# A third w_lo buffer in both stages of a hybrid decoder layer

## What is computed

```python
h = rms_norm(x, norm1_gain) * (1.0 + scale1) + shift1
proj = h @ w_in
(xa, ya, fq, fk, fv, ff, gq, gk, gv, glow, gg) = jnp.split(proj, ...)
out_a = rg_lru(causal_depthwise_conv(xa, conv_w, conv_b), ...) * jax.nn.gelu(ya)
out_b = forgetting_attention(fq, fk, fv, ff, fox_b_f, fox_q_gain, fox_k_gain)
out_c = gated_linear_attention(gq, gk, gv, glow, gg, ...)
mix = jnp.concatenate([out_a, out_b, out_c], axis=-1) @ w_out
x = x + gate1 * mix
h = rms_norm(x, norm2_gain) * (1.0 + scale2) + shift2
gt, up = jnp.split(h @ ffn_w_gate_up, 2, axis=-1)
x = x + gate2 * ((jax.nn.silu(gt) * up) @ ffn_w_down)
```

## Time and profile before

| | |
|---|---|
| median of 3 runs | 2975.97 us (2973.37 to 2981.22) |
| the profiled execution | 2978.72 us, span 2976.9 us |
| mean granted TensorE clock | 0.975 |
| TensorE busy | 2813.1 us (94%) |
| VectorE busy | 1464.6 us (49%) |
| ScalarE busy | 1185.6 us (40%) |
| GpSimd busy | 1036.4 us (35%) |

### The profile page before, as it was taken

The page is one execution under the profiler, slowest core; times in us unless marked ns, Lnnn a source line. Parts: engine busy times, 40 slices in busy tenths (PEclk is TensorE's granted clock), DMA queues, the critical chain, the costliest instruction groups (busy, mean ns, idle before and its releaser), DMA issues.

```text
span 2976.9 us, 32965 instructions
## 1 busy us (share of the span) xinstructions
PE 2813.1 (94%) x12416; PEld 2209.3 (74%) x12416; DVE 1464.6 (49%) x1876; ACT 1185.6 (40%) x1654; POOL 1036.4 (35%) x488
## 2 busy tenths in 40 slices
PE   8998998888989999999999999999999999999999
PEld 4786876566757787886777777867777777778887
DVE  3968786566554334445443454464445654521111
ACT  3333333343345354444433535454335455332222
POOL 2544454221324332233433222434331122444443
PEclk9999999889989999999999999999999999999999
DMA  7555545626643344444624444445244544423222
GB/s 268 181 157 190 152 140 155 184 82 171 212 130 126 121 122 138 127 152 138 185 82 127 144 139 138 148 149 179 70 142 139 155 147 124 141 92 99 93 99 92
DMA packets 159902, 419.05 MB, mean 141 GB/s; under 512 B 18284, under 2 KB 20604, under 8 KB 156672
## 3 DMA queue, kind: packets, MB, share of 16 engines
q1 hardware_dynamic: 157408, 412.48, 44.2%
q10 hardware_dynamic: 2336, 4.46, 0.4%
HBM read 355.95 MB, written 60.92 MB: 140 GB/s over the span
## 4 chain that ended last, share of the span: by engine, by line
PE 65%; DVE 6%; ACT 3%; issue 3%; DMA 2%; SPq 2%; POOL 1%; ACTq 0%; POOLq 0%; DVEq 0%
PE ff_acc_ps L77 17%; PE ff_acc_ps L78 17%; PE ff_acc_ps L79 17%; PE fa_st_ps L1691 1%; PE fa_s_ps L1665 1%; PE fa_o_ps L1707 1%; PE fa_st_ps L1692 1%; PE fa_s_ps L1666 1%; PE fa_o_ps L1709 1%; PE fa_o_ps L1708 1%; DVE fa_inv_sum L1408 1%; PE fa_st_ps L1744 1%; DVE ff_silu L1371 1%; PE fa_o_ps L1781 1%; SPq L956 1%
## 5 line engine op out<-in xcount | busy, mean ns | idle before, releaser
L1093 POOL TENSOR_TENSOR w_lo<-ff_w_raw,w_hi 128x1024 fp32r<-128x1024 f32 (+1 forms) x326 | 772.6, 2370 | 1614.6 <-PE ff_acc_ps L79 1537.6
L77 PE MATMUL ff_acc_ps<-h_odd_hi,w_hi 128*128 128x512 f32 x1856 | 750.2, 404 | 47.8 <-DVE h_odd_lo L1376 13.3
L78 PE MATMUL ff_acc_ps<-h_odd_lo,w_hi 128*128 128x512 f32 x1856 | 737.4, 397 | 0.0
L79 PE MATMUL ff_acc_ps<-h_odd_hi,w_lo 128*128 128x512 f32 x1856 | 735.9, 396 | 0.0
L1108 ACT ACTIVATE w_hi<-ff_w_raw 128x1024 fp32r<-128x1024 f32 (+1 forms) x326 | 338.8, 1039 | 928.7 <-PE ff_acc_ps L79 714.6
L77 PEld LDWEIGHTS ff_acc_ps<-h_odd_hi,w_hi 128*128 128x128 f32 x1856 | 356.8, 192 | 155.5 <-issue 62.5
L79 PEld LDWEIGHTS ff_acc_ps<-h_odd_hi,w_lo 128*128 128x128 f32 x1856 | 356.4, 192 | 78.0
L78 PEld LDWEIGHTS ff_acc_ps<-h_odd_lo,w_hi 128*128 128x128 f32 x1856 | 357.0, 192 | 72.8 <-issue 1.7
L1401 DVE TENSOR_TENSOR fa_p_lo<-fa_probs,fa_p_hi 128x512 fp32r<-128x512 f32 x240 | 154.4, 644 | 286.8 <-ACT fa_p_hi L1142 286.5
L77 PE MATMUL ff_acc_ps<-ff_a_hi,w_hi 128*128 128x512 f32 x704 | 285.2, 405 | 10.1 <-issue 6.1
L78 PE MATMUL ff_acc_ps<-ff_a_lo,w_hi 128*128 128x512 f32 x704 | 280.1, 398 | 0.0
(11 more groups left out here) (263 smaller groups left out, 4044.1 us busy)
## 6 DMA issues: line engine op xcount, KB each, us to landing
ff_w_raw<-in_w_gate_up SPq DMA_DIRECT2D x176, 512.0 KB, 4.0
w_raw<-in_w_in SPq DMA_DIRECT2D x74, 512.0 KB, 4.2
ff_w_raw<-in_w_down SPq DMA_DIRECT2D x64, 512.0 KB, 3.6
mod_w<-in_w_mod SPq DMA_DIRECT2D x24, 1024.0 KB, 5.3
fa_v<-v_split_dram SPq DMA_DIRECT2D x60, 384.0 KB
ff_w_raw<-in_w_out SPq DMA_DIRECT2D x32, 512.0 KB, 3.9
fa_ks_a<-ka_dram SPq DMA_DIRECT2D x60, 256.0 KB
fa_kt_a<-ka_dram SPq DMA_DIRECT2D x60, 256.0 KB
```

The lines of the kernel that those rows point to most:

```text
L77: nc.tensor.matmul(out, hi, act_hi, start=first, stop=False)
L78: nc.tensor.matmul(out, hi, act_lo, start=False, stop=False)
L79: return nc.tensor.matmul(out, lo, act_hi, start=False, stop=last)
L1093: nc.gpsimd.tensor_tensor(w_lo[:, j % LO, wide], w_raw[:, j % RAW, wide], w_hi[:, j % HI, wide].bitcast(F32), ALU.subtract).then_inc(lo_re ...
```

## The change

LO goes from 2 to 3 in both stages and `w_lo` gets three slots, 4096 more bytes in each partition. `high` and `low` stay as they are, and so do the numbers of all other buffers.

```diff
@@ project_in_and_recur
-    RAW, HI, LO, GB, MW, STAGES = 2, 3, 2, 3, 3, 3
+    RAW, HI, LO, GB, MW, STAGES = 2, 3, 3, 3, 3, 3
@@ mix_and_feed_forward
-    HI, LO, RAW, GB, SB, XR = 3, 2, 3, 2, 2, 12
+    HI, LO, RAW, GB, SB, XR = 3, 3, 3, 2, 2, 12
@@ build
-            ("h_odd_hi", [P, KD, BLK], F32R), ("h_odd_lo", [P, KD, BLK], F32R), ("w_hi", [P, 3, KD * P], F32R), ("w_lo", [P, 2, KD * P], F32R),
+            ("h_odd_hi", [P, KD, BLK], F32R), ("h_odd_lo", [P, KD, BLK], F32R), ("w_hi", [P, 3, KD * P], F32R), ("w_lo", [P, 3, KD * P], F32R),
```

## The result

The changed kernel takes 2986.8 us (median of 15 runs) against 2976.0 us (also 15 runs): a ratio of 1.0035, with a 95% interval of 1.0026 to 1.0044. The change costs about 10.4 us. Forecast were 2975.5 us, with a chance of 0.55 that the difference stays within 0.3%, and a range of 2958 to 2989 us. The time lies inside the range, but the forecast change was -0.5 us. The profiled execution of the changed kernel took 2986.6 us, with a span of 2984.8 us, 7.9 us more than the one before.

A forecast was written before the change was run, and what follows sets the result against it. TensorE was busy for 2813.1 of 2976.9 us, so a buffer could act only on the other 163.8. The terms -6.6 - 8.9 + 6.6 + 5.7 + 2.7 gave -0.5 us, hence 2975.5 us, range 2958 to 2989.

The forecast's parts named there:

- the fall by half in stage 1: Sign that the prediction is right: TensorE's waits on w_lo, 13.5 us in stage 1, fall by about half.
- The race in (a): Stage 2: VectorE's subtraction after the maxima's conversion gets in ahead of the moved split, by 0.06 us or somewhat more.
- (a): Columns of maxima, stage 2: six of 24 conversions no longer caught by a split, 1.49 us each, 8.9 us gained.
- (b): Attention slots: the later split delays VectorE work before piece maxima and maxima's columns, six waits of 1.1 us, 6.6 us lost.
- The median of a_lo: Sign in the attention slots: a_lo remainders slow from a median of 1.39 to about 2.5 us.
- (c): Next block's normalised input: the moved split delays the last two h_lo by 1.9 us at three block ends, 5.7 us lost.
- (d): Chain scaling q and k: saves 1.5 us, loses about 2.4, so 0.9 us in each of three blocks, 2.7 us lost.
- A term that was right only in part: stage 1: Waits on w_lo: mod_acc products run faster once the split precedes them, 2.2 us in each of three blocks, 6.6 us gained.
- The seven products at that place: Stage 1's mod_acc chain from 241.50: 7.66 us beside GpSimd, 3.61 beside it idle; 2.2 us expected back.
- The slower rival: The split takes the ports just ahead of the subtraction; six waits grow by 1.1 us: +15.0 us, 2991.0 us, chance 0.20.

The follow-up runs named there:

- the kernel with 15 late splits: Three buffers in both stages, but 15 of stage 2's 326 splits, at its start and three block starts, keep their old place: 2974.8 us (0.9985).
- the kernel with all other splits late: Three buffers in both stages; all stage-2 splits keep their old place except 15 at its start and three block starts: 2993.9 us (1.0043).
- the space alone: Against the kernel before, the third buffer's space is allocated but unused, with two buffers used in both stages: 2977.4 us (0.9997).

## Why the prediction failed

**What held.** The split moved behind ScalarE's copy, by a unit's wait replaced with 1.1 us, as described. The waits on w_lo stayed nearly as they were, at 15.1 and 7.5 us; the fall by half in stage 1, which the prediction named as a sign, did not come. The race in (a) was won: the subtraction starts 0.14 us ahead of the split, where the prediction had 0.06 "or somewhat more". Changed kernel:

```profile
1789.06 0.17 DVE L1393 CAST fa_m_cols<-fa_neg_max 128x4 fp32r<-128x4 f32 x1
1789.26 0.17 DVE L1395 TENSOR_TENSOR fa_m_cols<-fa_neg_max,fa_m_cols 128x4 fp32r<-128x4 f32 x1
```

```profile
1789.40 2.39 POOL L1093 TENSOR_TENSOR w_lo<-ff_w_raw,w_hi 128x1024 fp32r<-128x1024 f32 x1 [8.40 <-ACT w_hi L1108]
```

The busy time of the 24 conversions fell from 13.2 to 5.4 us, by 7.8 of the 8.9 forecast. TensorE's waits behind them fell by 4.7 us only, from 17.9 in 14 to 13.2 in 11. Taken one by one, the six waits of (a) fell by 1.5 us each, 9.0 in all, and five others grew or came new, by 4.4 in all: the loss of (b), which reached the columns of maxima too. With the 2.2 us on the piece maxima it comes to 6.6 us, the size forecast. The median of a_lo went from 1394 to 2468 ns, as forecast. The loss in (b) came at the place forecast. What VectorE did there in the changed kernel:

```profile
1809.37 2.35 DVE L1401 TENSOR_TENSOR fa_p_lo<-fa_probs,fa_p_hi 128x512 fp32r<-128x512 f32 x1
```

It took 1.26 us before, and TensorE's wait behind it grew from 0.91 to 2.00 us. (a) and (b) were put at -2.3 us together; the kernel with 15 late splits shows -1.2 for all of stage 2 but those places. (c) held in its wait: at the three block ends TensorE waits 1.6, 1.6 and 1.8 us longer, 5.0 us where 5.7 were forecast.

**The step that failed: term (d), and the clock that the sum left out.** (c) and (d) were put at 5.7 and 2.7 us, 8.4 together; the runs give 15 to 16, each with an error of 4 to 5. Two things are wrong. First, (d) counted one new collision per chain, "loses about 2.4" against 1.5 saved. Each chain met two. At two block starts L1577 ahead of it was caught as well, and at the start of stage 2 L1459 was, with nothing saved. TensorE's waits for the chain grew by 3.0, 1.9 and 1.6 us, 6.5 in all and not 2.7, and putting the splits around them back returned 9.5 us, with an error of 4. Second, and the same in (c): the price of a wait was taken as its length. No term stood for matmuls that get slower behind a longer wait, and at the three block starts TensorE's busy time grew by 5.5 us for the same matmuls, beside 7.9 us more idle time. The block start shown above costs 6.0 us, not 1.9 + 0.9. With measured terms the sum is -3.3 (stage 1) - 1.2 + 14.9 = +10.4 us. These three are differences along one row of kernels, so they must add up to the result; the independent figure for the last is the 16.1 us of the kernel with all other splits late.

**A term that was right only in part: stage 1.** Forecast -6.6 us, measured -3.3. Its first half came and its second didn't. The seven products at that place take 6.75 us (7.66 before), not 5.5, because the sums of squares and the next split came to lie beside them. But the product that opens the chain (L359) takes 0.34 us where it took 2.00, so the eight together are done 2.6 us sooner after their start, near the 2.2 forecast. The chains behind lose part of it again: the next but one takes 5.46 us for its seven where it took 4.49. And TensorE's wait doesn't follow: between 225 and 300 us it waits 7.2 us for splits (6.8 with stage 1's buffer alone), against 5.8 before. What disappears in stage 1 is another wait, in the changed kernel and in the one with stage 1's buffer alone. In the kernel before it is:

```profile
PE gate_ps L544 <- ACT lru_u_in L299: 4.3, 3, 2.2
```

It is still there with the space alone (3.9 us) and with stage 2's buffer alone (3.7). That it carries the 3.3 us is likely by its size, but was not tried by itself.

**The slower rival** had the race in (a), which was won. Its 2991 us is near the result for a reason that isn't the real one. The chance of 0.20 for slower rested on the race alone. It had no room for losses that are larger than their first collision and their wait.

## What to carry to other kernels

A further buffer that takes away a wait also moves the work that waited; where two engines exclude each other from SBUF, ask what it will lie beside, and count every instruction of a chain that it can catch, not the first, at each place where the chain stands. Cut a long GpSimd instruction into pieces before tuning its place: here pieces of 128 columns were worth 59 us (1.0035 to 0.9837), the buffer and its place 10 to 16. Price a growing TensorE wait by the stretch around it, with its clock, and not by its own length: at one block start 3.3 us of longer waits came to 6.0 us, and at the start of stage 2 a wait longer by 3.0 us came to 1.1.

## What the runs showed of the hardware

- A longer wait can lower the clock of the matmuls beside it, and need not. In the two profiles, the same piece of the program around (b), 189 matmuls, before and then after:

```profile
1800.10:1841.70 41.60, 40.37 (x189) 1.00 0.43 135
```

```profile
1796.50:1841.90 45.40, 42.01 (x189) 0.96 0.40 124
```

  Two waits grew there, that for the piece maximum from 0.91 to 2.00 us and one for a column of maxima from 0.32 to 1.40, so idle time grew from 1.2 to 3.4 us. The clock was 0.96, which is some time at 1.2 GHz, and the matmuls took 42.01 - 40.37 = 1.6 us longer. But four other kernels have the same two waits and a clock of 1.00. One of them is the kernel with stage 2's buffer alone (waits of 1.97 and 1.40 us):

```profile
1805.40:1849.20 43.80, 40.43 (x189) 1.00 0.40 128
```

  So the length of the wait alone doesn't decide it. What does was not tried.
- The exclusion works both ways. At 256 columns four pieces take 2.79 us in one place, where VectorE does nothing until the last of them. Beside VectorE's row work at a block start, whose instructions get in between, they take 4.81 us:

```profile
1385.76 4.81 POOL L1095 TENSOR_TENSOR w_lo<-ff_w_raw,w_hi 128x256 fp32r<-128x256 f32 x4 [2.84 <-ACT w_hi L1111]
...
1417.96 2.79 POOL L1095 TENSOR_TENSOR w_lo<-ff_w_raw,w_hi 128x256 fp32r<-128x256 f32 x4 [4.38 <-ACT w_hi L1111]
```

- Over the whole kernel, 2976 us long and 94% busy on TensorE, the length of one GpSimd instruction decides about 54 us: so much (0.9989 - 0.9809, with an error of about 6) is returned against the kernel with stage 1's buffer alone by cutting the split, with no work taken away, though GpSimd is busy for only 35% and VectorE for 49%. That most of it is what the two keep from each other is argued from the waits, which fall on VectorE's work all over stage 2; it was not counted one by one.
